# Copying a state buffer in eight pieces during a projection, and splitting the first weight block's low part in quarters

## The reference

```python
h = rmsnorm(x, g_attn_norm)              # 512 x 1024 (prompt), 8 x 1024 (samples)
z = h @ w_in                             # w_in: 1024 x 2840, float32
...
win_all = jnp.concatenate([win_buf, kv_w], axis=1)     # win_buf: (8, 512, 2, 2, 64), one new row each
new_win_kv_sample = win_all[:, W + T - n_keep:]         # rows 1..511 of the old state, then the new row
```

## Time and profile before

| | |
|---|---|
| median of 3 runs | 1145.65 us (1145.42 to 1149.24) |
| profiled execution | 1144.81 us, of which the span 1143.0 us |
| projection in that execution | first product at 17.39 us, last eviction at about 166 us |
| share of the span that an engine is busy | PE 93%, DVE 54%, ACT 34%, POOL 6% |
| granted TensorE clock, mean | 0.943 |

### The profile page before, as it was taken

One profiled execution on the slowest core, in us unless ns is written; L12 is line 12 of the kernel. 1 busy time (PEld: TensorE's weight loads), 2 busy tenths in 40 slices (PEclk: granted clock), 3 DMA queues, 4 the chain that ended last, 5 costly groups with the idle time before them and its releaser, 6 DMA issues.

```text
span 1143.0 us, 22964 instructions
## 1 busy us (share of the span) xinstructions
PE 1061.2 (93%) x8284; PEld 933.5 (82%) x8284; DVE 619.5 (54%) x1056; ACT 391.3 (34%) x729; POOL 63.3 (6%) x83
## 2 busy tenths in 40 slices
PE   6899998988989998899999889999999999998995
PEld 5899997887878886555555558999999999998995
DVE  5334664777768776775455445445533335553334
ACT  4111122333333335656454354322221112222124
POOL 1000003111111100000000000100000000000000
PEclk8899996989989895999998999999999999999998
DMA  8427539999999853356666762223333332333221
GB/s 295 151 89 201 129 98 227 250 248 258 269 261 260 246 182 120 121 175 226 204 208 194 214 203 75 75 74 92 110 92 91 92 83 84 91 92 93 90 78 75
DMA packets 180323, 177.59 MB, mean 155 GB/s; under 512 B 13128, under 2 KB 140869, under 8 KB 177893
## 3 DMA queue, kind: packets, MB, share of 16 engines
q1 hardware_dynamic: 178536, 169.72, 52.5%
q10 hardware_dynamic: 1724, 7.04, 1.8%
HBM read 170.83 MB, written 10.06 MB: 158 GB/s over the span
## 4 chain that ended last, share of the span: by engine, by line
PE 61%; SPq 18%; issue 7%; DVE 5%; DMA 5%; ACT 3%; ACTq 1%; POOL 0%; DVEq 0%; POOLq 0%
PE bank L664 59%; SPq L578 4%; SPq L499 3%; SPq L542 3%; SPq L545 3%; PE bank L668 3%; SPq L492 2%; DMA high_arena<-in_w_in_dram 2%; SPq L566 2%; DMA low_arena<-in_cache_nsa_slc_kv_dram 1%; DMA low_arena<-in_consts_dram 1%; DMA high_arena<-out_cmp_p_dram 1%; ACTq L1284 1%; DVE high_arena L2231 0%; DMA high_arena<-in_cache_nsa_slc_kv_dram 0%
## 5 line engine op out<-in xcount | busy, mean ns | idle before, releaser
L664 PE MATMUL bank<-high_arena 128*128 128x254 f32 (+8 forms) x1864 | 242.0, 349 | 11.9 <-ACT high_arena L1321 6.1
L664 PEld LDWEIGHTS bank<-high_arena 128*128 128x128 f32 (+5 forms) x1864 | 186.9, 153 | 49.8 <-issue 9.2
L2163 DVE TENSOR_TENSOR w_low<-high_arena,w_high 128x1024 fp32r<-128x1024 f32 x72 | 90.1, 1252 | 81.0 <-ACT w_high L1484 71.0
L1484 ACT ACTIVATE w_high<-high_arena 128x1024 fp32r<-128x1024 f32 x72 | 76.4, 1061 | 144.7 <-PE bank L664 144.7
L668 PE MATMUL bank<-low_arena 128*128 128x128 f32 (+3 forms) x658 | 103.2, 298 | 16.4 <-DMA low_arena<-in_cache_nsa_slc_kv_dram 10.4
L664 PE MATMUL bank<-a_high,w_high 128*128 128x256 f32 (+1 forms) x512 | 103.7, 284 | 5.3 <-issue 2.9
L668 PEld LDWEIGHTS bank<-low_arena 128*128 128x128 f32 (+3 forms) x658 | 83.0, 157 | 28.9 <-issue 12.3
L664 PE MATMUL bank<-h_high,w_high 128*128 128x256 f32 (+1 forms) x512 | 103.0, 282 | 1.8 <-DVE h_low L2187 1.8
L664 PE MATMUL bank<-a_low,w_high 128*128 128x256 f32 (+1 forms) x512 | 103.2, 283 | 0.0
L664 PE MATMUL bank<-h_low,w_high 128*128 128x256 f32 (+1 forms) x512 | 103.2, 283 | 0.0
L664 PE MATMUL bank<-h_high,w_low 128*128 128x256 f32 (+1 forms) x512 | 103.1, 283 | 0.0
(11 more groups left out here) (227 smaller groups left out, 1541.2 us busy)
## 6 DMA issues: line engine op xcount, KB each, us to landing
low_arena<-in_cache_sb_kv_dram SPq DMA_DIRECT2D x128, 256.0 KB, 4.8
high_arena<-in_cache_sb_kv_dram SPq DMA_DIRECT2D x128, 256.0 KB, 3.5
high_arena<-in_cache_nsa_cmp_kv_dram SPq DMA_DIRECT2D x128, 128.0 KB, 5.0
high_arena<-in_w_up_dram SPq DMA_DIRECT2D x32, 512.0 KB, 4.0
high_arena<-in_w_down_dram SPq DMA_DIRECT2D x32, 512.0 KB, 4.0
high_arena<-in_w_in_dram SPq DMA_DIRECT2D x10, 1136.0 KB, 5.9
low_arena<-in_cache_nsa_slc_kv_dram SPq DMA_DIRECT2D x128, 64.0 KB
high_arena<-in_cache_nsa_slc_kv_dram SPq DMA_DIRECT2D x128, 64.0 KB, 2.3
```

Of the source, the lines that this page charges most:

```text
L664: return T.matmul(out, lhsT=l, rhs=r, start=start, stop=stop, **k)
L1484: S.activation(w_hi_r[u], w_raw[u], ACT.Copy).then_inc(sem(f"w_hi{u}"), 1)
L2163: V.tensor_tensor(w_lo_r[u], w_raw[u], w_hi[u], ALU.subtract).then_inc(sem(f"w_lo{u}"), 1)
```

## The change

Three edits. (1) The eight copies of the sliding state are no longer issued in a row ahead of the loop over the blocks: each is issued on ACT's queue inside of the loop, one behind the two evictions of each of the blocks 0 to 7. (2) The first block's low part is made in quarters: slices 0 and 1 on DVE, ahead of its `gained_low` work, slices 2 and 3, 4 and 5, 6 and 7 on GpSimd, each signalled by itself. DVE's half of before goes away. (3) PE's waits follow: `w_lo0` at slice 0, `z_zero` at slices 2, 4 and 6.

```diff
                     if begin:
                         pe.wait_ge(sem("hT_ev"), k + 1)
                         if k == 0:
-                            pe.wait_ge(sem("z_zero"), 2)
-                        if k == KD // 2:
                             pe.wait_ge(sem("w_lo0"), 1 + 1)
+                        elif k % 2 == 0:
+                            pe.wait_ge(sem("z_zero"), k // 2 + 1)
...
             wb, wo = A["state_nsa_win_kv"][0], O["win_s"][0]
-            for b in range(B):
-                act.dma_start(wo[b, 0:WIN - 1].rearrange("(o s) k h d -> o (s k h d)", o=1),
-                    wb[b, 1:WIN].rearrange("(o s) k h d -> o (s k h d)", o=1)).then_inc(sem("kv_out"), 16)
+            def window_rows(b):
+
+                act.dma_start(wo[ds(b, 1), 0:WIN - 1].rearrange("o s k h d -> o (s k h d)"),
+                    wb[ds(b, 1), 1:WIN].rearrange("o s k h d -> o (s k h d)")).then_inc(sem("kv_out"), 16)
+
             for turn, turns, col in COLUMNS:
                 more = turn + turns < NCB // 2
                 with act.Fori(0, turns if more else turns - 1) as i:
                     win_high(1, i + turn)
                     z_out(0, i, turn, col)
+                    window_rows(i * 2 + 2 * turn)
                     win_high(0, i + turn + 1)
                     z_out(1, i, turn, col)
+                    window_rows(i * 2 + (2 * turn + 1))
                 if not more:
                     win_high(1, NCB // 2 - 1)
...
             for t in range(2, NT):
                 row_scale(t, t + 2)
+            dve.wait_ge(*signal("w_hi_first", 1))
+            V.tensor_tensor(win_r[0][:, 0:2], win[0][:, 0:2], win_hi[0][:, 0:2], ALU.subtract).then_inc(sem("w_lo0"), 1)
             for k in range(KD):
                 gained_low(k)
-                if k == 2:
-                    dve.wait_ge(sem("w_hi0"), 1)
-                    V.tensor_tensor(win_r[0][:, KD // 2:], win[0][:, KD // 2:], win_hi[0][:, KD // 2:], ALU.subtract).then_inc(sem("w_lo0"), 1)
             dve.wait_ge(sem("z_zero"), 1)
...
             G_.memset(z[:, NT, :], 0.0).then_inc(sem("z_zero"), 1)
             pool.wait_ge(*signal("w_hi_first", 1))
-            G_.tensor_tensor(win_r[0][:, 0:KD // 2], win[0][:, 0:KD // 2], win_hi[0][:, 0:KD // 2], ALU.subtract).then_inc(sem("z_zero"), 1)
+            G_.tensor_tensor(win_r[0][:, 2:4], win[0][:, 2:4], win_hi[0][:, 2:4], ALU.subtract).then_inc(sem("z_zero"), 1)
+            pool.wait_ge(sem("w_hi0"), 1)
+            G_.tensor_tensor(win_r[0][:, 4:6], win[0][:, 4:6], win_hi[0][:, 4:6], ALU.subtract).then_inc(sem("z_zero"), 1)
+            G_.tensor_tensor(win_r[0][:, 6:8], win[0][:, 6:8], win_hi[0][:, 6:8], ALU.subtract).then_inc(sem("z_zero"), 1)
```

## The result

The changed kernel takes 1153.43 us (median of 9 runs, 1150.03 to 1161.78) against 1145.65 us (9 runs, 1142.09 to 1151.17). The ratio is 1.0065 with an interval of 1.0036 to 1.0095: slower by 7.4 us (4.1 to 10.9). The forecast was 1148 us, range 1139 to 1159, with slower by over 0.5% at 0.34 and no change at 0.48. The measured time lies inside the range, but above the 1145 to 1151 of the likeliest case: the loss was over twice the 3.1 us of the sum.

What follows compares the result with a forecast made beforehand. PE, busy for 93% of the span, was taken to bound the kernel; 8.9 us of new waits less 5.8 gained by block 2 made 3.1 us slower than the profiled 1144.8, so 1148 us, range 1139 to 1159.

Steps and rivals of the forecast that it cites:

- the likeliest case: Whole kernel: the prediction's own sum holds, 1148 us, spanning 1145 to 1151; chance 0.40.
- the sum: Projection: 8.9 us more waiting at the samples less 5.8 gained by block 2, 3.1 us slower.
- The start: First block's low part in quarters: PE starts near 16.1, 1.3 us earlier; 0.8 us gained, bounds 0.1 and 1.5.
- The copies leave the front: ACT's queue: block 1's high part starts near 23.7, block 2's load is issued near 35.1, without the 1.7 us delay.
- A piece beside a load: Loads of blocks 2 to 9: each copy issued beside one delays its landing 1.6 us, bounds nothing and 3.2.
- The rule on the closing write: DMA engines: a semaphore write lands only after earlier writes across queues, so a load delay near the upper end is likelier.
- What PE feels: PE's samples, seven loads from 55.80 on: 7 x 1.6 less 2.3 of slack, 8.9 us more waiting.
- gained by block 2: Block 2's samples: start 2.9 us earlier, after a 0.8 us wait, and 2.9 from half clock gone; 5.8 us gained.
- The pieces do not hide: Rival judged, at the loads: copies overlap them, delay 0.5 us or less, time 1139.5 us; chance 0.24.
- The clock can fall at the new waits: Rival at the samples of blocks 2 to 9: 2.9 us per fall, 1157 us for three falls; chance 0.25.
- GpSimd did not go first: Rival judged, at the start: GpSimd's quarter precedes DVE's, gain falls from 0.8 to about 0.1, 1148.6 us; chance 0.05.
- The costly copy: Rival at the loads: a copy costs more than its engine time, 2.2 us each, or its issue does; 1152.7 us, chance 0.06.

Runs made afterwards that it cites:

- cut pair: Two kernels ended behind the projection, all later work left out, compared: quarters only against before -0.1 us, changed against before +5.6 us.
- kernel without copies: Changed kernel with the copies of the 511 old rows left out, that output not written: ratio 0.9952 to the kernel before.
- pieces between the loads: Changed kernel with each copy issued behind a block's high part, once that block's load has landed: ratios 0.9969 and 0.9966 to the kernel before.
- cut kernel with pieces between the loads: Changed kernel with each copy issued once the block's load has landed, ended behind the projection: 162.79 us, -3.8 to before ended there.
- cut kernel: A kernel ended behind the projection, all later work left out: the kernel before 166.55 us, the changed kernel 172.19 us.
- cut kernel of before: Kernel before the change, ended behind the projection, nothing after the last eviction of z done: median 166.55 us.
- cut kernel with quarters only: Changed kernel with the eight copies back ahead of the loop, ended behind the projection: 166.46 us, -0.1 to before ended there.

## Why the prediction was right or wrong, point by point

**The start.** Mostly right. PE began at 16.09 (16.1 was said). DVE went first, at 14.58; GpSimd's first quarter, begun at 14.63, took 1.96 us, against 1.39 and 1.40 for the others, which ran beside other work of DVE. This agrees with the lock of the Trainium skill (SBUF — State Buffer, section SBUF: two separate sides): the later starter took about 0.6 us longer beside DVE's quarter of 0.75 us. It was hidden, as the sum had it. The clock fell later and came back sooner (0.50 from about 18.6 to 22.0, where it was 17.0 to 23.8), so PE was about 1.5 us ahead at the first tile's end, not 0.8. In all four profiled executions with the old start half clock lasted some 6.8 us there; of the ten with the quarters it lasted some 3.4 us in three, and seven had none. Why, no run here shows. But the quarters by themselves are worth nothing (-0.1 us in the cut pair, within its spread): I counted their 0.8 us without asking what is late next when the copies stay. With the copies moved they may count: without them the changed kernel would be 1.7 to 2.5 us slower by the ratios (1.0080 against 1.0065 and 1.0058), which is not clear of noise.

**The copies leave the front.** Right: ACT's high part at 23.74 (23.7 was said), the load of block 2 at 34.74 (35.1).

**A piece beside a load.** Right in kind, 15% high in size: 1.6 us was said, 1.39 measured, in proportion to the bytes, and gone when the two don't meet. This agrees with the rule weighed in the prediction, of the Trainium skill (DMA: Bandwidth & Descriptors, section Issuing engines are not separate DMA queues): the piece came from another queue than the load and held it up all the same. The rule on the closing write is neither borne out nor excluded: by it a delay near the upper end, 3.2 us, was likelier, and 1.39 was measured.

**What PE feels.** Right in total, and that in part by luck, since two misses cancel. The seven waits are 7.5 us, of which 0.4 was there before; 8.9 more was said. With the measured 1.39 the same working gives 7 x 1.39 - 2.3 = 7.4. Block 2 waits 2.32 us, not 0.8: PE was there 0.7 us earlier than said (40.72), and its load took 8.3 us (34.74 to 43.04), where 7.1 was said. Without a piece beside it this load took 7.1 us in the kernel without copies and 5.9 in the one with pieces between the loads, where the next took 5.5; why it is slower stays open. Together the pieces cost 9.4 us in the cut pair that differs in nothing but their place (172.19 less 162.79), where the prediction had 8.9 + 0.8 = 9.7.

**The step that failed** is the term "gained by block 2", 5.8 us with its own wait, 6.7 without: the cut kernel with pieces between the loads shows the latter as 3.8. What is missing is the 2.9 us for half clock behind block 2's samples. The rest of the term, 0.8 + 3.0, is there: the samples start at 41.28 against 45.27, 4.0 us earlier, with the clock at 1.00 behind both. The 2.9 was read off one execution of before, and I priced it as certain; the same stretch cost 2.7 us in that execution, 1.5 in another and nothing in the cut kernel. With 3.8 in place of 6.7, the sum of 3.1 becomes 9.7 - 3.8 = 5.9 us. That the cut pair shows 5.6 tests only the 9.7 in it, as 5.6 is the difference of the measured 9.4 and 3.8. In the first pair of executions, where the fall was there, the projection ended 2.6 us later and 3.1 was said; there the waits that came out smaller and the gain that did (block 2 started 2.2 us earlier, not 2.9) cancel in part.

**Rivals.** The pieces do not hide. The clock can fall at the new waits, as the place said, but it fell in two places of one execution and in none of the other, and in the cut kernel at one place of one run in six; it is scatter on top, not the cause. GpSimd did not go first. The costly copy, at 1152.7 us, is near the measured time, but its condition failed: a piece cost less than its engine time, not more. The rest of the kernel is not shown to take part: 7.4 and 6.6 less 5.6 is within the intervals, and the time behind the projection, 986.8 and 984.1 us, is that of the kernel with pieces between the loads, 986.1 and 984.4. That the first execution of before ended its projection at 165.65 and the cut one at 163.39 is for the most part the fall of the clock behind block 2, 2.7 us; later waits of 0.61 and 0.24 us in the cut one, against 0.37, take about 0.5 of it back.

## What to carry to other kernels

A background copy has no cost of its own that shows here; it costs where it meets a load that the critical engine waits for, in proportion to its bytes. Tie its issue to the *landing* of that load, not to the event that starts the next one: the same eight pieces, one step earlier in the loop, turned 5.6 us lost into 3.8 gained in the projection alone. Moving a wait away gains only as far as the next thing that is late: the earlier start went into the wait for block 2's load. And a term that is read off one execution, a clock that fell above all, needs a second look before it goes into a sum at full price.

## What the runs showed of the hardware that was not expected

A wait does not by its length alone decide the granted clock. In two executions of one kernel, waits of 2.32 and 1.51 us left it at 1.00, and waits of 2.04 and 2.08 us at the same two places took it to 0.50 for the work behind them. And half clock is not always lost time: in the cut kernel of before PE ran at 0.50 for some 6.8 us at the start, and its samples of block 2 began at 45.27 us, where those of the cut kernel with quarters only, which had no half clock there, began at 45.01: both waited for the load.
